# Two expert layers with row gathers: sixteen gathers of each layer go in two parts

## The reference, cut to what matters

```python
def peer(h, w_query, sub_keys, expert_u, expert_v):      # T = 256 tokens, D = 1024
    q = (hf @ w_query).reshape(T, PEER_HEADS, 2, PEER_HALF)             # 8 heads
    scores = jnp.einsum("thpd,hpnd->thpn", q, sub_keys)                 # 128 keys on each side
    top_v, top_i = lax.top_k(scores, PEER_TOPK)                         # 16 of each side
    cand_v = top_v[:, :, 0, :, None] + top_v[:, :, 1, None, :]
    cand_i = top_i[:, :, 0, :, None] * PEER_NKEYS + top_i[:, :, 1, None, :]
    best_v, best_pos = lax.top_k(cand_v.reshape(...), PEER_TOPK)        # 16 of the 256 sums
    expert_idx = jnp.take_along_axis(cand_i, best_pos, axis=-1)         # of 16384 experts
    gates = jax.nn.softmax(best_v, axis=-1)
    ...
    u = jnp.take(expert_u, idx, axis=0)                                 # one row of 1024 each
    vv = jnp.take(expert_v, idx, axis=0)
    a = jax.nn.gelu(jnp.einsum("td,thkd->thk", h, u))
    return jnp.einsum("thk,thkd->td", g * a, vv)
```

## Time and profile before

| | |
|---|---|
| runs | 2362.08 us median of 3 (2357.12 to 2362.88) |
| the profiled execution | 2355.88 us, its span 2354.3 us |
| mean granted TensorE clock | 0.964 |
| PE busy, VectorE busy | 2108.5 us (90%), 1601.0 us (68%) |
| ScalarE busy, GpSimd busy | 804.7 us (34%), 569.4 us (24%) |
| DMA | 772.80 MB, mean 328 GB/s |

### The profile page before, as it was taken

One profiled execution on the slowest core, in us unless ns is written; L12 is line 12 of the kernel. 1 busy time (PEld: TensorE's weight loads), 2 busy tenths in 40 slices (PEclk: granted clock), 3 DMA queues, 4 the chain that ended last, 5 costly groups with the idle time before them and its releaser, 6 DMA issues.

```text
span 2354.3 us, 25003 instructions
## 1 busy us (share of the span) xinstructions
PE 2108.5 (90%) x8854; PEld 1365.7 (58%) x8854; DVE 1601.0 (68%) x3312; ACT 804.7 (34%) x1741; POOL 569.4 (24%) x611
## 2 busy tenths in 40 slices
PE   8899999999999999998788777999999986887787
PEld 6688877788888765553333333687664542333333
DVE  7678854688967467765776675656586577667755
ACT  5644454544445422222122213355232212221222
POOL 0100010000003024333333333002143433333331
PEclk9999999999999999999998999999999999999999
DMA  7188933488853579999999999854699999999997
GB/s 289 72 304 322 346 124 117 181 317 322 322 189 144 185 274 413 421 421 421 421 421 422 421 421 421 342 197 170 222 393 422 421 422 421 421 421 421 421 422 302
DMA packets 161355, 772.80 MB, mean 328 GB/s; under 512 B 12983, under 2 KB 13367, under 8 KB 89566
## 3 DMA queue, kind: packets, MB, share of 16 engines
q0 software_dynamic: 80640, 587.24, 60.6%
q1 hardware_dynamic: 80606, 184.17, 21.7%
HBM read 770.27 MB, written 1.10 MB: 328 GB/s over the span
## 4 chain that ended last, share of the span: by engine, by line
DMA 29%; PE 28%; DVE 5%; issue 2%; ACT 1%; POOL 0%; DVEq 0%; POOLq 0%; ACTq 0%
DMA ring<-in_experts_uv_dram,experts_at 16%; PE experts_first L3179 9%; PE experts_fourth L3179 8%; DMA experts_v_slot<-in_experts_uv_dram,experts_at 8%; DMA experts_spare<-in_experts_uv_dram,experts_at 4%; PE experts_fourth L3160 2%; PE mix_sums L233 2%; PE mix_sums L235 1%; PE mix_sums L234 1%; PE experts_first L3133 1%; PE experts_second L3133 1%; DVE ring L2845 1%; PE experts_first L3160 1%; DMA shared<-in_experts_uv_dram,experts_at 1%; ACT experts_diagonal L3030 1%
## 5 line engine op out<-in xcount | busy, mean ns | idle before, releaser
L3030 ACT ACTIVATE experts_diagonal<-ident,experts_weight 128x128 f32<-128x128 f32 x488 | 155.9, 390 | 633.1 <-DVE experts_weight L2900 626.8
L2646 POOL DMA_INDIRECT ring<-in_experts_uv_dram,experts_at x248 | 237.6, 958 | 383.5 <-PE experts_first L3179 197.1
L228 DVE TENSOR_TENSOR early_w_lo<-ring,early_w_hi 128x1024 fp32r<-128x1024 f32 x196 | 245.0, 1260 | 97.0 <-ACT early_w_hi L2296 53.6
L3179 PE MATMUL experts_first<-ring,experts_diagonal 128*128 128x512 f32 x560 | 267.9, 628 | 47.8 <-ACT experts_diagonal L3030 47.8
L3179 PE MATMUL experts_fourth<-ring,experts_diagonal 128*128 128x512 f32 x432 | 218.8, 658 | 57.4 <-ACT experts_diagonal L3030 57.4
L2845 DVE CUSTOM_DVE_ANT_0 ring<-ring,experts_third 128x1024 f32<-128x1024 f32 x140 | 170.5, 1218 | 100.3 <-DMA ring<-in_experts_uv_dram,experts_at 99.5
L3179 PEld LDWEIGHTS experts_first<-ring,experts_diagonal 128*128 128x128 f32 x560 | 109.7, 201 | 187.7 <-issue 128.0
L3179 PE MATMUL experts_fourth<-experts_v_slot,experts_diagonal 128*128 128x512 f32 x368 | 181.6, 638 | 37.6 <-ACT experts_diagonal L3030 35.1
L3179 PEld LDWEIGHTS experts_fourth<-ring,experts_diagonal 128*128 128x128 f32 x432 | 89.2, 211 | 182.7 <-issue 115.0
L2845 DVE CUSTOM_DVE_ANT_0 ring<-ring,experts_second 128x1024 f32<-128x1024 f32 x108 | 131.7, 1220 | 89.5 <-DMA ring<-in_experts_uv_dram,experts_at 86.9
L2845 DVE CUSTOM_DVE_ANT_0 experts_v_slot<-experts_v_slot,experts_second 128x1024 f32<-128x1024 f32 x92 | 112.2, 1220 | 87.1 <-DMA experts_v_slot<-in_experts_uv_dram,experts_at 87.0
(11 more groups left out here) (547 smaller groups left out, 4689.4 us busy)
## 6 DMA issues: line engine op xcount, KB each, us to landing
mlp_ada_rows<-in_ada_turned_dram POOLq DMA_DIRECT2D x48, 1024.0 KB, 8.2
ring<-in_w_in_dram SPq DMA_DIRECT2D x19, 2048.0 KB, 8.8
ring<-in_mlp_w_in_dram SPq DMA_DIRECT2D x16, 2048.0 KB, 11.2
ring<-in_mlp_w_out_dram SPq DMA_DIRECT2D x16, 2048.0 KB, 10.3
ring<-in_gla_w_in_dram SPq DMA_DIRECT2D x6, 2048.0 KB, 8.4
ring<-in_w_out_dram SPq DMA_DIRECT2D x4, 2048.0 KB, 7.6
ring<-in_w_query_dram SPq DMA_DIRECT2D x4, 2048.0 KB, 8.5
experts_v_slot<-in_w_query_dram SPq DMA_DIRECT2D x4, 2048.0 KB, 13.3
```

Of the source, the lines that this page charges most:

```text
L228: return dve.tensor_tensor(out_lo, a, hi.bitcast(F32), ALU.subtract)
L2646: pool.indirect_dma_start(pair(i), None, rows, bass.IndirectOffsetOnAxis(ap=at[:, n, j:j + 1], axis=0)).then_inc(pair_in[slot[i]], 16)
L3030: act.activation(diagonal[:, i % TOPK, :], K.ident[:], ACT.Copy, scale=weight[:, n, i % TOPK:i % TOPK + 1]).then_inc(diagonal_ready, 1)
L3179: mm = pe.matmul(y[n // PH][:, b, :], diagonal[:, j, :], v_row(i)[:, b * HALF:(b + 1) * HALF], start=n % PH == 0 and j == 0, stop=False, s ...
```

## The change

In each of the two expert stages, unit 13 (`IN_TWO = UNITS - 3`) gets its sixteen gathers in two parts: rows 0 to `CUT` - 1, and the rest. `CUT` is 120 in the first layer and 124 in the second. The second part reads its row numbers from `at_far`, whose first partitions hold a copy of `at[CUT:P, 13, :]`: SP makes that copy with a DMA once the numbers of unit 13 are there and its rows have landed, and GpSimd waits for it ahead of the first second part. Both parts add 16 to `pair_in`, so `pair_arrived` counts 16 more for each gather of unit 13 that a place has held.

```diff
+    IN_TWO, CUT = UNITS - 3, 120 if out is None else 124
...
+    at_far = st.sb("at_far", [P, TOPK], U32)
...
     def pair_arrived(i):
-        return 16 * (filled[i] + 1)
+        return 16 * sum(1 + (j // TOPK == IN_TWO) for j in uses[slot[i]][0:filled[i] + 1])
...
         for source, there in zip(row_sources, row_places):
             sp.dma_start(there, source).then_inc(rows_there, 16)
+        sp.wait_ge(at_ready, IN_TWO + 1)
+        sp.wait_ge(rows_there, 16 * ROWS)
+        sp.dma_start(at_far[0:P - CUT, :], at[CUT:P, IN_TWO, :]).then_inc(rows_there, 16)
...
         def gather(i):
             n, j = divmod(i, TOPK)
+            if n != IN_TWO:
+                pool.indirect_dma_start(
+                    pair(i), None, rows,
+                    bass.IndirectOffsetOnAxis(ap=at[:, n, j:j + 1], axis=0)).then_inc(pair_in[slot[i]], 16)
+                return
             pool.indirect_dma_start(
-                pair(i), None, rows,
-                bass.IndirectOffsetOnAxis(ap=at[:, n, j:j + 1], axis=0)).then_inc(pair_in[slot[i]], 16)
+                pair(i)[0:CUT, :], None, rows,
+                bass.IndirectOffsetOnAxis(ap=at[0:CUT, n, j:j + 1], axis=0)).then_inc(pair_in[slot[i]], 16)
+            if j == 0:
+                pool.wait_ge(rows_there, 16 * ROWS + 16)
+            pool.indirect_dma_start(
+                pair(i)[CUT:P, :], None, rows,
+                bass.IndirectOffsetOnAxis(ap=at_far[0:P - CUT, j:j + 1], axis=0)).then_inc(pair_in[slot[i]], 16)
```

## The result

The changed kernel takes 2475.84 us (median of 6 runs, 2466.99 to 2478.41), the kernel before 2361.20 beside it (6 runs, 2356.88 to 2366.2): 1.0482 times the time [1.0464 to 1.05], 114.6 us more. The prediction was 2358 us with a range to 2400. The profiled execution has a span of 2473.6 us, 119.3 more than that of before.

A forecast was written before the change was run, and what follows sets the result against it. The 16 DMA engines set the pace; the split saves 1.2 + 3.1 = 4.3 us at the two stage ends, all else nothing: 2355.9 - 4.3 = 2351.6 profiled, 2358 us on the runs' median, range 2350 to 2400.

The forecast's parts named there:

- What bounds the kernel: Expert stages: the 16 DMA engines set the pace at about 421 GB/s; earlier landings at stage ends pass on one for one.
- eight rows to an engine in order: Unit 13's long parts: eight rows per engine in order, 0.311 us each; the sixteenth gets none of 120, four of 124.
- few engines: Rival: unit 13's 124-row parts go to four engines, 31 rows each, 9.6 us a part; chance 0.25 together with collisions.
- two groups of four, 8 of the 16 on each: Second layer's long parts alternate between two groups of four engines: 248 rows against 128, +37 us, 2399.
- The rival on the other side: Unit 13's parts go to few engines (+37 us, or 114 on the same four), or engines collide (80 us); chance 0.25.
- full collisions: Two engines write through one path, so unit 13's rows take twice as long: 39.8 us a layer, 80 in all.
- Relief of the late engine: Two stage ends: the split takes rows off the late engine, 1.2 + 3.1 = 4.3 us less; chance 0.36.
- no relief: Rival: a moving deal skips another engine each time, or the late one isn't the sixteenth; 0 to +2 us, chance 0.22.
- The zeros: Terms for small packets, GpSimd's extra issues, and SP's copy with its wait: each taken to cost nothing.
- GpSimd: A pair of issues for unit 13 takes 2.48 us, covered by some 13 us of queued work: nothing lost.
- Small packets: One more per engine for each extra gather, 16 a layer: between nothing and 5.0 us a layer, taken as nothing.
- SP and the copy: SP's copy to at_far takes 2 to 18.3 us, within 42 us before unit 13's first gather: nothing lost.

The follow-up runs named there:

- long_alone: Changed kernel with unit 13's short parts left out, only 120 rows fetched in the first layer and 124 in the second: 2517.14 us.
- low_half: Changed kernel with unit 13 fetching only rows 0 to 63, in one part, in both layers: 2379.39 us, against 2361.97 for the kernel before.
- middle_half: Changed kernel with unit 13 fetching only rows 32 to 95, in one part, in both layers: 2337.38 us, against 2361.97 for the kernel before.
- second_alone: Changed kernel with only the second layer split (124 and 4 rows), the first layer's gathers whole: 2423.75 us, 1.0261 times the kernel before.
- cut64: Changed kernel with unit 13's gathers cut at 64 rows in both layers, two parts of 64: 2433.05 us, 1.0297 times the kernel before.

## Why the prediction was wrong

**What bounds the kernel** held: the engines set the pace, and what the queue lost inside the two units (48.9 and 67.3 us by its rate) came out at the stages' ends (50.8 and 70.6).

**The failed step** is how a part's rows are dealt, "eight rows to an engine in order", with each row at 0.311 us. The prediction said that it rested most on this, and both halves failed.

- *First layer.* 15 of 16 engines get rows, as I had it, but not the same 15 each time, and a row takes 0.546 us in place of 0.312 with the long part alone. With 120 rows over 16 engines in the long run, 7.5 each, that is 16 gathers x (7.5 x 0.546 - 8 x 0.312) = 26 us of the 32.0 that *long_alone* lost; the other 6 aren't accounted for. The short part then adds 13 to 19 (45.2 and 50.8 less 32.0). That a row's time hangs on which partitions a part covers is shown by *low_half* against *middle_half*. That it is pairs of engines at one inlet in the cuts at 120 and 124 too is argued from there, and not shown: which rows of a part go to which engine the trace doesn't say.
- *Second layer.* 124 rows go to four engines with 31 each. The rival "few engines" had this down to the "two groups of four, 8 of the 16 on each", for +37 us; its rows were to cost 0.311. In *second_alone* the stage lost 64.0: the mechanism is shown, and the term is short by 5 us for rows of 0.331 in the middle and by 22 for the slow rows around it (0.46 to 0.74 us). In the change itself rows take 0.48 us from 2280 to 2300 as well, and it is 70.6.

**The rival on the other side** was the right one, as alternatives of which one would do. Two came together: slow rows in both layers, which it priced at 39.8 us a layer, and few engines in the second. *cut64*, the plain case of slow rows, has 39.9 and 35.2. That the first meets the price so closely is in part luck, as a row takes 1.8 times as long there (0.561 against 0.312) and not twice. 39.8 in each layer and 37 would have been 117 us; it was 121. The range ended at 2400 because I took these as alternatives and gave full collisions too little.

**Relief of the late engine**, 4.3 us of gain: none. With 15 engines of 16 and a moving start, each is left out equally often, as the rival "no relief" had it. The first layer's last gathers after, 1 us each, against the earlier trace rows:

```profile
1541.00:1542.00 1.00, 1.00 (x3) 0.19 (x1) 0.73 (x3) 0.20 (x1) 0.00 (x0) 1.00 0.06 25
...
1543.00:1544.00 1.00, 1.00 (x4) 0.38 (x2) 1.00 (x2) 0.00 (x0) 0.00 (x0) 1.00 0.06 25
1544.00:1545.00 1.00, 0.51 (x3) 0.01 (x1) 0.23 (x3) 0.60 (x2) 0.00 (x0) 1.00 0.04 16
```

One engine alone again (0.06). The engines' adds for the stage's last gather say it outright: before, the fifteenth came at 1492.8 and the sixteenth at 1496.6; after, at 1541.5 and 1545.3, 3.8 us behind in both. In the second layer first and last were 9.0 us apart before (2333.0 and 2342.0) and 10.8 after (2450.5 and 2461.3). Which engine it is stays open, and so does whether a split could be fitted to it.

**The zeros.** GpSimd: right, 2.46 us a pair against my 2.48, and idle for 12 us at a stretch; the second layer's 124-row issues, at some 1.27 us, changed nothing. Small packets: nothing, as I had it, at 8 to 22 ns, though there are 6400 more in the second layer and not 256. SP and the copy: right, the copy is issued at 1316.2 in the first layer, 45 us ahead of the first gather that needs it (1361.16), and no wait for it stands in the table:

```profile
L2630 SPq DMA_DIRECT2D experts_at_far<-experts_at x2: 627/700/773, 1316.2 to 2212.2; - x2
```

**Still open.** Two groups of four engines hardly slow each other (*second_alone*, 331 ns in the middle) and four groups do by four times (*long_alone*, 1268 ns); how they come into step or stay out of it the runs don't show. No split that was tried and fetches all rows beats the kernel before.

## What to carry to other kernels

A full DMA share says that the engines are busy, not that they move data: read it beside GB/s, and where the share is full at half the rate, look at which partitions the parts of a transfer cover. Before cutting a transfer by partitions, count two things: the largest divisor up to 16 of each part's rows, which is how many engines it gets here, and how many of the inlets of the map above its partitions reach. If a transfer of all 128 partitions has to be cut, cut it by columns: here that cost 2 us a layer against 35 to 71.

## What the runs showed of the hardware that wasn't expected

- Half of a gather can take longer than the whole: 64 rows into partitions 0 to 63 made the stage 12.1 us longer, the same number into 32 to 95 made it 10.5 us shorter.
- A gather of 124 rows runs on four engines. Sixteen of them alone, with four rows fewer to load in each, cost 130.5 us; the four-row gathers added behind them gave 60 to 66 us of it back.
- Engines without rows get a 4-byte packet for each row step: 372 more in a gather of 124 rows, about 8 ns each.
- An indirect gather's issue on GpSimd depends on its number of rows in an odd way: 0.94 us for 128, 0.97 for 120, some 1.27 for 124, 0.88 for 8 and 4.
- PE's granted clock fell to 0.50 and 0.51 of full speed (the lower of its two levels, 1.2 GHz) where it had had nothing or little to do, and eight matmuls that free places took 6.39 us (3.2 a gather against 1.98). In *low_half* and *cut64*, too, it fell in just these stretches (0.66 and 0.67), where PE waited for late landings; what these slower matmuls add to the loss wasn't measured apart.
- The 16 engines drift apart over a stage of whole gathers. Before, in the second layer, the first and the last engine's adds for one gather are 3.0 us apart at 1953, 4.0 at 1980, 5.0 at 2035, 6.0 at 2090, 7.0 at 2172 and 7.9 at 2226: the late engine falls back in steps of about 1 us.
